# Gated feed-forward rows turned in blocks of 32 by 32 by VectorE, instead of by TensorE

## The chip, the cores and the metric

The kernel runs on one core of one Trainium2 chip. The metric is the device time of one execution in microseconds; the median of several runs counts. The engines named below are TensorE (PE in the profile; PEld is its weight load), VectorE (DVE), ScalarE (ACT), GpSimd (POOL) and SyncE (SP), which only issues DMAs here. Operands lie in SBUF, matmul results in PSUM, which has eight banks of 512 fp32 values on each of 128 partitions.

## The reference

Two transformer-like blocks, one behind the other, over 256 tokens with 2048 channels, in fp32. The first has two layers, each with a mixer, a cross-attention and a gated feed-forward. Only the feed-forward matters here:

```python
FFN_HIDDEN = ((8 * D_MODEL + 3 * 256 - 1) // (3 * 256)) * 256     # 5632

def swiglu(h, w_in, w_out):
    g, u = jnp.split(h @ w_in, 2, axis=-1)
    return (jax.nn.silu(g) * u) @ w_out

# in each of the 2 layers of the first block
x = x + swiglu(rms_norm(x, norm_ffn[i]), ffn_w_in[i], ffn_w_out[i])
```

## The kernel before

Every linear layer is done in split precision: a weight tile w becomes w_hi (rounded to fp32r, by ScalarE, L388) and w_lo = w - w_hi (by VectorE, L395), and activations are split likewise. Three products are added up: hi x w_hi, lo x w_hi (L949) and hi x w_lo (L956). Weights come in units of 2 x 128 rows by 512 columns (512 KB), loaded by SP (L376). Four slots (NS = 4) of w_raw, w_hi and w_lo go round: while TensorE works on unit u, ScalarE and VectorE make w_hi and w_lo of unit u + 4 as soon as TensorE has released unit u (semaphore w_used), and SP loads into a w_raw slot once VectorE's split of it is done (w_lo_done). One unit is 8 matmuls with w_hi and 4 with w_lo.

The first half of the feed-forward, `fin0` and `fin1`, runs over 11 blocks of 512 hidden columns (NH = 11) in each of the two layers. A block is 16 units: eight for the gate (b = 0, PSUM banks 0 and 1), eight for the up projection (b = 1, banks 2 and 3). Behind the gate ScalarE writes silu of it to sg (L995). Behind the block VectorE multiplies it with the up projection into hid (L1025): tokens on the partitions, 2 x 512 values each. The second half, `fout0` and `fout1`, needs the hidden columns on the partitions, so hid is turned. That happens one block later, beside the matmuls of the next block: TensorE turns the eight 128 x 128 tiles of hid into banks 4 and 5 after unit 2 of the gate (`transposes`, L918 to L925), ScalarE copies them out rounded to hidT_hi behind its split of unit 4 (`hi_part`, L976), and VectorE makes hidT_lo behind its own (`lo_part`, L1007). The semaphores are hid_done, ht_done (turned), ht_hi_done and ht_lo_done. Block 0 is written out; blocks 1 to 10 are one hardware loop on each engine (`turn_c`). What is left over of block 10 is handed to the next stage by `owed` and done at the given unit of it by `pay`, here in units 2 and 4 of the down projection; that one takes its unit j (b = 0) once ht_lo_done has reached block j // 2 + 1, so block 10's columns are wanted at units 20 and 21.

Each engine works through its instructions in order, so the order written in `pe_ffn`, `act_ffn` and `dve_ffn` is the order of execution.

Of the kernel before, what the change touches and what calls it, by code (L numbers as in the profile page):

```python
# [12 lines left out]
P = 128  # L13
SEQ = 256
TB = SEQ // P
# [30 lines left out]
def program(nc, a):  # L46
    ctx = ExitStack()
    with ctx:
        def sem(name):
            return ctx.enter_context(nc.semaphore(name))  # L50
# [10 lines left out]
        def new(name, shape, dt=F32):  # L61
            off = top[0]
            top[0] += (4 * int(np.prod(shape)) + 31) // 32 * 32
            assert top[0] <= base + slab_bytes, (name, top[0] - base - slab_bytes)
            return at(name, shape, off, dt)
# [9 lines left out]
        hid = new("hid", [TB, CB])  # L75
# [48 lines left out]
        ident = new("ident", [P])  # L124
# [49 lines left out]
        ps = ctx.enter_context(nc.psum_tensor("ps", [P, 8, 512], F32))  # L174
# [32 lines left out]
        hid_done = sem("hid_done")  # L207
        ht_done = sem("ht_done")
# [140 lines left out]
        owed = dict(pe=[], act=[], dve=[])  # L349

        def pay(who, j):
            for at_, work in owed[who]:
                if at_ == j:
                    work()
            owed[who] = [(at_, work) for at_, work in owed[who] if at_ != j]
# [34 lines left out]
        def dve_split(dve, us, i=0, body=0, first=False):  # L390
            v = us if first else us + NS
            if v >= NU:
                return
            dve.wait_ge(w_hi_done, v + 1 + i * body)
            nc.vector.tensor_tensor(w_lo[:, v % NS], w_raw[:, v % NS], w_hi[:, v % NS].bitcast(F32),  # L395
                                    ALU.subtract).then_inc(w_lo_done, 1)
# [28 lines left out]
        def tiles(t, k_off=0):  # L425
            return lambda k, tb: t[:, k + k_off, tb * P:(tb + 1) * P]
# [425 lines left out]
        def dve_add_out(dve, name, turned, mid=None):  # L852

            li = L[name]
            pool = name == "pool"

            def evac(i, b, used):
                e = block_no(name, i, b)
                dve.wait_ge(w_used, used)
                if pool:  # L860
                    dve.wait_ge(pscale_in, 16)
                if not (pool and b < 2):

                    dve.wait_ge(x_copied, XB0[name] + e - 1)
                c0 = b * CB if pool else li.cols(i)[b]
                xb = x[:, :, bass.ds(c0, CB)]
                if pool:
                    sc = pscale[:, c0:c0 + CB].rearrange("p (o n) -> p o n", o=1).broadcast_to([P, TB, CB])
                    vlink(nc.vector.tensor_tensor(stg[b % 2][:], acc(half_of(name, b)), sc, ALU.mult))
                    nc.vector.tensor_tensor(stg[b % 2][:], xb, stg[b % 2][:], ALU.add).then_inc(stg_done, 1)  # L870
                else:
                    nc.vector.tensor_tensor(stg[b % 2][:], xb, acc(half_of(name, b)), ALU.add).then_inc(stg_done, 1)
                dve.wait_ge(stg_done, XB0[name] + e + 1)
                dve.sem_inc(acc_free[half_of(name, b)], 1)
            split_turns(dve, dve_split, name, evac, mid, turn_x=lambda i, b: dve_turn_x(dve, name, turned, i, b))
# [28 lines left out]
        NH = HID // CB  # L904

        def turn_c(eng, l, body):

            body(0, True)
            with eng.Fori(1, NH) as i:
                body(i, False)  # L910
# [3 lines left out]
        def pe_ffn(pe, l):  # L914
            li = L[f"fin{l}"]
            h0 = NH * l

            def transposes(i):  # L918
                pe.wait_ge(hid_done, h0 + i)

                for j in range(4):
                    for h in range(TB):
                        mm = nc.tensor.transpose(ps[:, 4 + j // 2, (j % 2) * SEQ + h * P:(j % 2) * SEQ + (h + 1) * P],  # L923
                                                 hid[:, h, j * P:(j + 1) * P], ident[:])
                mm.then_inc(ht_done, 1)  # L925

            def body(i, first):
                for b in range(2):
                    if b == 0:
                        if first:  # L930
                            pe.wait_ge(acc_free[0], half0[f"fin{l}"][0])
                        else:
                            pe.wait_ge(silu_done, h0 + i)
                    else:
                        if first:
                            pe.wait_ge(acc_free[1], half0[f"fin{l}"][1])
                        else:
                            pe.wait_ge(hid_done, h0 + i)
                    for j in range(li.units):
                        us = li.u0 + b * li.units + j  # L940
                        s = us % NS
                        pe.wait_ge(w_hi_done, us + 1 + i * li.body)
                        if first and b == 0:
                            pe.wait_ge(t_lo_done, TS[f"ffn{l}"][0] + j + 1)
                        for kk in range(UK):
                            k = UK * j + kk
                            for tb in range(TB):
                                for part, lhs in enumerate((actT_hi, actT_lo)):
                                    nc.tensor.matmul(  # L949
                                        ps[:, 2 * b + tb], lhs[:, k, tb * P:(tb + 1) * P],  # L950
                                        w_hi[:, s, kk * CB:(kk + 1) * CB], start=(k == 0 and part == 0), stop=False)
                        pe.wait_ge(w_lo_done, us + 1 + i * li.body)
                        for kk in range(UK):
                            k = UK * j + kk
                            for tb in range(TB):
                                mm = nc.tensor.matmul(  # L956
                                    ps[:, 2 * b + tb], actT_hi[:, k, tb * P:(tb + 1) * P],
                                    w_lo[:, s, kk * CB:(kk + 1) * CB], start=False, stop=(k == KT - 1))
                        mm.then_inc(w_used, 1)
                        if b == 0 and j == 2 and not first:  # L960
                            transposes(i)
                        if b == 0 and first:
                            pay("pe", j)
            turn_c(pe, l, body)
            owed["pe"].append((2, lambda: transposes(NH)))
            pe.wait_ge(silu_done, h0 + NH)
            pe_linear(pe, f"fout{l}", tiles(hidT_hi), tiles(hidT_lo), ht_lo_done, lambda b, j: h0 + min(NH, j // 2 + 1),
                      turned=AFTER_FFN[l])
# [32 lines left out]
        def dve_ffn(dve, l):  # L1001
            li = L[f"fin{l}"]
            h0 = NH * l

            def lo_part(i):
                dve.wait_ge(ht_hi_done, h0 + i)
                nc.vector.tensor_tensor(hidT_lo[:, bass.ds(4 * i - 4, 4)],  # L1007
                                        ps[:, 4:6].rearrange("p b (j t) -> p (b j) t", j=2),
                                        hidT_hi[:, bass.ds(4 * i - 4, 4)].bitcast(F32), ALU.subtract)\
                    .then_inc(ht_lo_done, 1)  # L1010

            def body(i, first):
                for b in range(2):
                    for j in range(li.units):
                        dve_split(dve, li.u0 + b * li.units + j, i, li.body)
                        if b == 0 and j == 4 and not first:
                            lo_part(i)
                        if b == 0 and first:
                            pay("dve", j)
                dve.wait_ge(silu_done, h0 + 1 + i)  # L1020
                dve.wait_ge(w_used, li.u0 + (i + 1) * li.body)
                if not (l == 0 and first):
                    dve.wait_ge(ht_done, h0 + i)
                for tb in range(TB):
                    ins = nc.vector.scalar_tensor_tensor(out=hid[:, tb], in0=ps[:, 2 + tb], scalar=rx[:, tb:tb + 1],  # L1025
                                                         in1=sg[:, tb], op0=ALU.mult, op1=ALU.mult)
                ins.then_inc(hid_done, 1)
            turn_c(dve, l, body)
            owed["dve"].append((4, lambda: lo_part(NH)))
            dve_add_out(dve, f"fout{l}", AFTER_FFN[l])  # L1030

        i_turned = sem("i_turned")
# [1359 lines left out]
```

## Time and profile before

| | before |
|---|---|
| median of 3 runs | 3051.22 us (3050.28 to 3053.83) |
| profiled execution, its own time | 3052.06 us |
| its span | 3050.2 us |
| TensorE busy | 3014.4 us (99%) |
| VectorE busy | 1692.0 us (55%) |
| ScalarE busy | 1478.4 us (48%) |
| GpSimd busy | 276.0 us (9%) |
| granted TensorE clock, mean | 0.999 of full speed |

The span goes from the first to the last instruction. Busy time of an engine is the time in which at least one of its instructions runs; matmuls are pipelined, so their durations overlap, and how long one holds the queue is read from the distance of two starts. Idle time of an engine stands in brackets behind the instruction that ended it, with what released it.

### The profile page before, as it was taken

How to read it: one execution, taken by the hardware profiler on the slowest of the kernel's cores; microseconds unless marked ns; L12 is line 12 of the kernel's file. 1: busy time of each engine (PE TensorE's matmuls, PEld its weight loads, DVE VectorE, ACT ScalarE, POOL GpSimd, SP SyncE). 2: the span in 40 equal slices, each digit the busy share in tenths (PEclk: the TensorE clock that was granted, in tenths of full speed). 3: DMA queues.
4: the chain of work that ended last, by engine and by line, in shares of the span. 5: the costliest groups of instructions: out<-in, count | busy, mean ns of one | idle time of the engine just before them, and what ended most of it. 6: DMA issues, size and time to landing. Idle time of an engine off the chain costs nothing.

```text
span 3050.2 us, 38222 instructions
## 1 busy us (share of the span) xinstructions
PE 3014.4 (99%) x14184; PEld 2489.1 (82%) x14184; DVE 1692.0 (55%) x1778; ACT 1478.4 (48%) x1839; POOL 276.0 (9%) x269
## 2 busy tenths in 40 slices
PE   8999999999999999999999999999999999999999
PEld 7888888888888778888888888888887888888787
DVE  5654444544456855654444545457556555755654
ACT  6554444444445555544444444454555545455553
POOL 0110000000005421100000000004200000600000
PEclk9999999999999999999999999999999999999999
DMA  7666666666666546566666656566454455644455
GB/s 251 220 186 191 187 192 186 188 189 191 190 193 188 149 127 220 172 191 190 186 192 186 189 189 191 190 196 190 146 152 138 150 183 178 187 145 145 144 156 170
DMA packets 280736, 549.45 MB, mean 180 GB/s; under 512 B 16896, under 2 KB 18976, under 8 KB 280224
## 3 DMA queue, kind: packets, MB, share of 16 engines
q1 hardware_dynamic: 276352, 531.30, 57.7%
q0 software_dynamic: 4256, 16.40, 1.5%
q8 instruction: 85, 1.39, 0.2%
q14 instruction: 43, 0.35, 0.0%
HBM read 540.82 MB, written 6.82 MB: 180 GB/s over the span
## 4 chain that ended last, share of the span: by engine, by line
PE 93%; ACT 3%; DVE 2%; issue 1%; POOL 1%; DMA 1%; ACTq 0%; DVEq 0%; POOLq 0%
PE ps L454 22%; PE ps L949 21%; PE ps L510 13%; PE ps L462 11%; PE ps L956 10%; PE ps L481 7%; PE ps L1179 1%; PE ps L1090 1%; DVE w_lo L395 1%; ACT w_hi L388 1%; PE ps L1157 1%; PE ps L783 1%; PE ps L923 1%; PE ps L1065 1%; DMA w_raw<-xattn_w_kv 0%
## 5 line engine op out<-in xcount | busy, mean ns | idle before, releaser
L395 DVE TENSOR_TENSOR w_lo<-w_raw,w_hi 128x1024 fp32r<-128x1024 f32 x1008 | 1275.0, 1267 | 1314.6 <-ACT w_hi L388 1311.1
L388 ACT ACTIVATE w_hi<-w_raw 128x1024 fp32r<-128x1024 f32 x1008 | 1066.8, 1059 | 1466.7 <-PE ps L462 584.8
L949 PE MATMUL ps<-w_hi,actT_hi 128*128 128x512 f32 x1408 | 550.0, 391 | 0.0
L949 PE MATMUL ps<-w_hi,actT_lo 128*128 128x512 f32 x1408 | 547.9, 389 | 0.0
L510 PE MATMUL ps<-w_hi,actT_hi 128*128 128x512 f32 x960 | 389.5, 406 | 5.7 <-ACT pall L534 5.7
L956 PE MATMUL ps<-w_lo,actT_hi 128*128 128x512 f32 x1408 | 376.5, 389 | 0.0
L510 PE MATMUL ps<-w_hi,actT_lo 128*128 128x512 f32 x960 | 375.2, 391 | 0.0
L454 PE MATMUL ps<-w_hi,hidT_hi 128*128 128x512 f32 x864 | 319.5, 391 | 0.0
L956 PEld LDWEIGHTS ps<-w_lo,actT_hi 128*128 128x128 f32 x1408 | 264.3, 188 | 55.1
L949 PEld LDWEIGHTS ps<-w_hi,actT_lo 128*128 128x128 f32 x1408 | 264.4, 188 | 54.2
L949 PEld LDWEIGHTS ps<-w_hi,actT_hi 128*128 128x128 f32 x1408 | 264.4, 188 | 54.1
L454 PE MATMUL ps<-w_hi,hidT_lo 128*128 128x512 f32 x736 | 286.4, 389 | 0.0
L481 PE MATMUL ps<-w_lo,actT_hi 128*128 128x512 f32 x960 | 262.5, 390 | 0.0
L510 PEld LDWEIGHTS ps<-w_hi,actT_hi 128*128 128x128 f32 x960 | 180.8, 188 | 47.3 <-issue 9.4
L462 PE MATMUL ps<-w_lo,hidT_hi 128*128 128x512 f32 x800 | 214.0, 389 | 0.0
L481 PEld LDWEIGHTS ps<-w_lo,actT_hi 128*128 128x128 f32 x960 | 180.2, 188 | 39.0
L510 PEld LDWEIGHTS ps<-w_hi,actT_lo 128*128 128x128 f32 x960 | 181.0, 188 | 34.1 <-issue 0.5
L454 PEld LDWEIGHTS ps<-w_hi,hidT_hi 128*128 128x128 f32 x864 | 161.8, 188 | 33.3 <-issue 0.3
L462 PEld LDWEIGHTS ps<-w_lo,hidT_hi 128*128 128x128 f32 x800 | 150.2, 188 | 31.3
L454 PE MATMUL ps<-w_hi,actT_hi 128*128 128x512 f32 (+1 forms) x416 | 161.4, 388 | 2.1 <-ACT w_hi L388 2.1
L454 PEld LDWEIGHTS ps<-w_hi,hidT_lo 128*128 128x128 f32 x736 | 138.2, 188 | 28.3
L454 PE MATMUL ps<-w_hi,actT_lo 128*128 128x512 f32 (+1 forms) x416 | 160.4, 386 | 0.0
(299 smaller groups left out, 2835.3 us busy)
## 6 DMA issues: line engine op xcount, KB each, us to landing
w_raw<-ffn_w_in SPq DMA_DIRECT2D x352, 512.0 KB, 3.6
w_raw<-w_in SPq DMA_DIRECT2D x256, 512.0 KB, 3.6
w_raw<-ffn_w_out SPq DMA_DIRECT2D x176, 512.0 KB, 3.8
w_raw<-w_out SPq DMA_DIRECT2D x64, 512.0 KB, 3.7
w_raw<-attn_w_in SPq DMA_DIRECT2D x48, 512.0 KB, 3.7
w_raw<-xattn_w_kv SPq DMA_DIRECT2D x32, 512.0 KB, 6.1
w_raw<-attn_w_out SPq DMA_DIRECT2D x32, 512.0 KB, 3.7
w_raw<-xattn_w_q SPq DMA_DIRECT2D x16, 512.0 KB, 3.7
```

The lines of the kernel that those rows point to most:

```text
L388: nc.scalar.activation(w_hi[:, v % NS], w_raw[:, v % NS], ACT.Copy).then_inc(w_hi_done, 1)
L395: nc.vector.tensor_tensor(w_lo[:, v % NS], w_raw[:, v % NS], w_hi[:, v % NS].bitcast(F32), ALU.subtract).then_inc(w_lo_done, 1)
L454: nc.tensor.matmul(ps[:, 2 * half + tb, 0:li.width], lhs(ks[kk], tb), w_hi[:, s, c:c + li.width], start=(j == 0 and kk == 0 and part == 0) ...
L462: mm = nc.tensor.matmul(ps[:, 2 * half + tb, 0:li.width], hi(ks[kk], tb), w_lo[:, s, c:c + li.width], start=False, stop=(j == li.units - 1 ...
L481: mm = nc.tensor.matmul(ps[:, 2 * half + tb], hi(k, tb), w_lo[:, s, kk * CB:(kk + 1) * CB], start=False, stop=(k == KT - 1))
L510: nc.tensor.matmul(ps[:, 2 * half + tb], lhs(k, tb), w_hi[:, s, kk * CB:(kk + 1) * CB], start=(k == 0 and part == 0), stop=False)
L783: mm = nc.tensor.transpose(ps[:, 4 + 2 * p + c, o:o + P], stg[p][:, h, k * P:(k + 1) * P], ident[:])
L923: mm = nc.tensor.transpose(ps[:, 4 + j // 2, (j % 2) * SEQ + h * P:(j % 2) * SEQ + (h + 1) * P], hid[:, h, j * P:(j + 1) * P], ident[:])
L949: nc.tensor.matmul(ps[:, 2 * b + tb], lhs[:, k, tb * P:(tb + 1) * P], w_hi[:, s, kk * CB:(kk + 1) * CB], start=(k == 0 and part == 0), sto ...
L956: mm = nc.tensor.matmul(ps[:, 2 * b + tb], actT_hi[:, k, tb * P:(tb + 1) * P], w_lo[:, s, kk * CB:(kk + 1) * CB], start=False, stop=(k == ...
L1065: mm = nc.tensor.transpose(ps[:, psum + col // 512, col % 512:col % 512 + P], src, ident[:])
L1090: mm = nc.tensor.matmul(o, un["q"][h], un["k"][h], start=un["row"] is None, stop=un["row"] is None or h >= 2)
```

## The change

VectorE turns hid, TensorE no longer does. VectorE's transpose works on blocks of 32 x 32. One instruction takes the 32 tokens of one quarter a of the partitions and the 32 columns of quarter f of each 128-column tile (for 4 tiles and 2 halves of the tokens: 8 blocks), turns each block and writes it to the partitions of quarter f in banks 4 and 5, at the columns of quarter a. Four such instructions (f = 0 to 3) make a quarter, four quarters a block. The quarters stand behind VectorE's splits of units 0 to 3 of the next block; the last one raises ht_done. `lo_part` moves from behind the split of unit 4 to that of unit 6. ScalarE's `hi_part` stays where it is. VectorE no longer waits for ht_done before it writes hid. For the last block of a layer the quarters are handed to units 0 to 3 of the down projection, and `lo_part` to its unit 6.

```diff
@@ pe_ffn
-            def transposes(i):
-                pe.wait_ge(hid_done, h0 + i)
-
-                for j in range(4):
-                    for h in range(TB):
-                        mm = nc.tensor.transpose(ps[:, 4 + j // 2, (j % 2) * SEQ + h * P:(j % 2) * SEQ + (h + 1) * P],
-                                                 hid[:, h, j * P:(j + 1) * P], ident[:])
-                mm.then_inc(ht_done, 1)
-
...
-                        if b == 0 and j == 2 and not first:
-                            transposes(i)
                         if b == 0 and first:
                             pay("pe", j)
             turn_c(pe, l, body)
-            owed["pe"].append((2, lambda: transposes(NH)))
@@ dve_ffn
+            def turn_quarter(i, a):
+                if a == 0:
+                    dve.wait_ge(hid_done, h0 + i)
+                for f in range(4):
+                    ins = nc.vector.transpose(
+                        ps[32 * f:32 * f + 32, 4:6].rearrange("p b (k h t) -> p h (b k) t", k=2, h=TB)
+                        [:, :, :, 32 * a:32 * a + 32],
+                        hid[32 * a:32 * a + 32].rearrange("p h (k n) -> p h k n", k=4)[:, :, :, 32 * f:32 * f + 32])
+                if a == 3:
+                    ins.then_inc(ht_done, 1)
+
...
-                        if b == 0 and j == 4 and not first:
+                        if b == 0 and j < 4 and not first:
+                            turn_quarter(i, j)
+                        if b == 0 and j == 6 and not first:
                             lo_part(i)
...
-                if not (l == 0 and first):
-                    dve.wait_ge(ht_done, h0 + i)
...
-            owed["dve"].append((4, lambda: lo_part(NH)))
+            for a_ in range(4):
+                owed["dve"].append((a_, lambda a_=a_: turn_quarter(NH, a_)))
+            owed["dve"].append((6, lambda: lo_part(NH)))
```

## Rows read from the trace of the kernel before

**Rows 1.** The page: busy time, chain that ended last by engine, one load.
```profile
span 3050.2 us, 38222 instructions
PE 3014.4 (99%) x14184; PEld 2489.1 (82%) x14184; DVE 1692.0 (55%) x1778; ACT 1478.4 (48%) x1839; POOL 276.0 (9%) x269
PE 93%; ACT 3%; DVE 2%; issue 1%; POOL 1%; DMA 1%; ACTq 0%; DVEq 0%; POOLq 0%
w_raw<-ffn_w_in SPq DMA_DIRECT2D x352, 512.0 KB, 3.6
```

**Rows 2.** By stretch: busy us (instructions) of PE, PEld, DVE, ACT, POOL; clock; DMA share; GB/s.
```profile
224.00:662.00 438.00, 438.00 (x1974) 363.46 (x1973) 217.45 (x189) 188.32 (x188) 0.00 (x0) 1.00 0.65 189
662.00:853.00 191.00, 191.00 (x856) 158.44 (x855) 94.25 (x83) 76.98 (x78) 2.09 (x2) 1.00 0.61 191
1293.00:1730.00 437.00, 437.00 (x1970) 362.66 (x1969) 217.56 (x193) 190.06 (x190) 0.00 (x0) 1.00 0.65 190
1730.00:1920.00 190.00, 190.00 (x852) 157.56 (x851) 94.98 (x83) 78.10 (x81) 2.09 (x2) 1.00 0.60 190
```

**Rows 3.** TensorE in order of time, 228 to 236 us: start, duration, instruction.
```profile
228.79 1.07 PE L956 MATMUL ps<-w_lo,actT_hi 128*128 128x512 f32 x4
...
231.51 1.07 PE L956 MATMUL ps<-w_lo,actT_hi 128*128 128x512 f32 x4
232.42 1.03 PE L923 MATMUL ps<-ident,hid 128*128 128x128 f32 x8
...
235.12 1.07 PE L956 MATMUL ps<-w_lo,actT_hi 128*128 128x512 f32 x4
```

**Rows 4.** VectorE in order of time, first layer; in brackets idle time before.
```profile
181.41 1.66 DVE L818 SCALAR_TENSOR_TENSOR actT_lo<-ps,gcols,actT_hi 128x256 fp32r<-128x256 f32 x4
...
226.75 1.40 DVE L1025 SCALAR_TENSOR_TENSOR hid<-ps,rx,sg 128x512 f32<-128x512 f32 x2
228.27 1.23 DVE L395 TENSOR_TENSOR w_lo<-w_raw,w_hi 128x1024 fp32r<-128x1024 f32 x1
...
240.04 1.23 DVE L395 TENSOR_TENSOR w_lo<-w_raw,w_hi 128x1024 fp32r<-128x1024 f32 x1 [1.49 <-ACT w_hi L388]
241.18 1.22 DVE L1007 TENSOR_TENSOR hidT_lo<-ps,hidT_hi 128x1024 f32 x1
242.76 1.23 DVE L395 TENSOR_TENSOR w_lo<-w_raw,w_hi 128x1024 fp32r<-128x1024 f32 x1 [0.36 <-ACT w_hi L388]
```

**Rows 5.** All instructions of line 923: duration ns min/median/max, first and last start.
```profile
L923 PE MATMUL ps<-ident,hid x176: 270/272/273, 232.4 to 1774.0; 128*128 128x128 f32 x176
```

**Rows 6.** VectorE in order of time, second layer, the last two blocks' hid.
```profile
1723.11 1.40 DVE L1025 SCALAR_TENSOR_TENSOR hid<-ps,rx,sg 128x512 f32<-128x512 f32 x2
...
1767.53 1.40 DVE L1025 SCALAR_TENSOR_TENSOR hid<-ps,rx,sg 128x512 f32<-128x512 f32 x2
```

**Rows 7.** VectorE's groups by shape: count, busy us, mean ns of one.
```profile
L1486 DVE COPY pall<-ps 128x256 f32<-128x256 f32 x8 | 3.3, 417 | 0.0
L818 DVE SCALAR_TENSOR_TENSOR actT_lo<-ps,gcols,actT_hi 128x256 fp32r<-128x256 f32 x80 | 33.1, 476 | 0.0
L641 DVE TENSOR_SCALAR xn<-x,rr 128x2048 f32<-128x2048 f32 x2 | 2.5, 1284 | 0.0
L630 DVE TENSOR_SCALAR nv<-ss 128x2 f32<-128x2 f32 x10 | 1.6, 165 | 2.3 <-ACT xn L601 2.3
L1860 DVE RECIPROCAL rr<-rt 128x32 f32<-128x32 f32 x6 | 2.1, 344 | 0.0
L1186 DVE RECIPROCAL rsum<-sums 128x4 f32<-128x4 f32 x24 | 4.0, 168 | 0.0
```

**Rows 8.** ScalarE in order of time, 225 to 250 us.
```profile
227.17 1.07 ACT L388 ACTIVATE w_hi<-w_raw 128x1024 fp32r<-128x1024 f32 x1 [1.60 <-PE ps L956]
...
239.91 1.01 ACT L976 ACTIVATE hidT_hi<-ps 128x1024 f32 x1
```

**Rows 9.** SyncE's waits, 224 to 760 us: us in total, times, longest us.
```profile
SPq L376 <- DVE w_lo L395: 413.8, 193, 3.0
```

## The prediction

> **What bounds the kernel now.** I read the page first [rows 1]. TensorE is busy 99% of the span at the full 2.4 GHz level, and holds 93% of the chain that ended last; VectorE is busy 55%, ScalarE 48%, so VectorE has room on average. An average says nothing about one stage, so the second view was the busy time by stretch [rows 2]: both stretches of the loop over hidden columns (224 to 662 us and 1293 to 1730 us), and both stretches of the down projection behind it, show TensorE busy without a gap, VectorE for 217.45 of 438 us. Whatever is taken off TensorE's queue there comes off the end, unless a wait grows in its place. The third view, TensorE's instructions in order of time [rows 3], shows what the transposes cost it. A unit is 12 matmuls and takes 2.72 us (231.51 - 228.79, start of the low part to start of the next). The unit with the eight transposes takes 3.61 (235.12 - 231.51). The transposes start right behind the fourth L956 matmul and had waited for nothing: hid was written at 226.75 to 228.15 [rows 4].
>
> **What is removed.** The 0.27 us of one transpose [rows 5] is its latency, not its place in the queue; 176 times that would be 48 us and wrong. The place in the queue is 3.61 - 2.72 = 0.89 us for eight. The same over a whole block of 16 units, from one hid to the next: in the second layer 1767.53 - 1723.11 = 44.42 us [rows 6]; 16 x 2.72 = 43.52; the difference is 0.90 us. I take 0.90. There are 176 transposes [rows 5], in groups of eight: 22 groups (11 blocks in each of 2 layers; the 11th group of a layer stands in unit 2 of the down projection). 22 x 0.90 = 19.8 us, all on a path without gaps.
>
> The wait of VectorE for ht_done before it writes hid goes too. It cost nothing: TensorE's transposes follow hid by some 5 us [rows 3, 4] and the next hid comes only a block later.
>
> **What is added.** VectorE gets 16 transposes for each block, in four quarters behind the split (w_lo) of units 0 to 3. One instruction reads 32 partitions x 256 values of SBUF and writes 32 x 256 into PSUM. No row of before shows a VectorE transpose, nor VectorE writing PSUM. Bounds by rows [rows 7]: the cheapest per element is the one-source scalar operation, 1284 ns for 2048 values; at that slope from 165 ns for 2 values 256 values take 0.30 us. The dearest is the reciprocal, 344 ns for 32 values and 168 ns for 4, so 6.3 ns a value and 1.8 us for 256. The nearest in kind is the copy between PSUM and SBUF with one source and 256 values, 0.42 us, then the two-source operation of the same size, 0.48 us, which stands in the queue for (1.66 - 0.476)/3 = 0.39 us when four follow each other [rows 4]. I take 0.45 us a piece, as four in a row may not overlap like those; the range to keep is 0.30 to 1.8.
>
> The rows put one value at about 1 ns for an operation of this kind: 1.22 us for 1024 values [rows 4] against 0.417 for 256 [rows 7] is 1.04 ns a value. The Trainium skill has two rules here that point apart. Its table of rules for kernel authors (VectorE: DVE Perf Modes) gives a 128 x 128 transpose to TensorE and keeps VectorE for 32 x 32; its page Vector Engine (DVE) Microarchitecture Reference (section 3.8) has the 32 x 32 array sustain one element a cycle in each lane, and lets an instruction of at most 32 partitions write to any quarter. By the second, a piece costs what the copy costs and the sum below stands; by the first, the sixteen pieces are the dearer way, which is the first rival.
>
> **Where it goes on VectorE.** Zero is the moment when ScalarE starts w_hi behind unit 0, 227.17 [rows 8]. VectorE starts its split of unit 0 at +1.10 (228.27) and an operation behind a split can start 1.14 later (241.18 - 240.04) [rows 4]. So a unit costs VectorE 1.14 + 4t, with t the time of one piece: 2.94 us at 0.45, against TensorE's 2.72. It falls behind by 0.2 us a unit, for four units, and catches up afterwards. The last quarter ends at 1.10 + 4 x 1.14 + 16t = 5.66 + 16t = 12.9 us. Who waits for that:
> - ScalarE, in hi_part behind w_hi of unit 4, is ready at 4 x 2.72 + 1.07 = 12.0. It waits 0.9 us, then 1.01 for hi_part [rows 8], and starts the next w_hi at 13.9 instead of 13.6. Queued behind its wait are the w_hi of the units to come.
> - VectorE's own split of unit 4 is late by 1 us; lo_part moves from unit 4 to unit 6, and its reader, the down projection, wants the last block's part only at its unit 20.
> - SP's loads wait for a free w_raw, which VectorE's split releases [rows 9]: late by 1 us as well, with 3.6 us to land [rows 1].
>
> None of it reaches TensorE, because four slots are in flight. The split behind unit 0 makes w_lo of unit 4, wanted at 3 x 2.72 + 8 x 0.227 = 9.97 us. For the split behind unit 4, the worst one, it is 20.85, and it ends at 5.66 + 16t + 1.23 = 6.89 + 16t: 14.1 us at 0.45, 6.7 us early. ScalarE's w_hi of unit 9 ends at 5.66 + 16t + 1.01 + 1.07 = 7.74 + 16t and is wanted at 21.76. Both covers last to t = 0.87 us. A load let go at 14.1 lands at 17.7, and ScalarE wants it at 21.76; that cover is thinner (4 us) but ScalarE has 7 us more behind it. The added work on VectorE (16 x 0.45 x 22 = 158 us) is therefore costed at nothing.
>
> **The sum.** Profiled span 3050.2 - 19.8 = 3030.4; the profiled execution took 3052.06, 1.9 more than its span, so 3032.3. The median of the runs is 3051.22, 0.84 below that execution: 3031.4 us, 0.65% less. In the other stages nothing is edited, and the work before and behind moves up as a whole.
>
> **Rivals.**
> - A piece takes far more than a copy (slower). From t = 0.87 the queue of splits comes too late: TensorE stands in each block for 16 x (t - 0.87), 352 x (t - 0.87) us over both layers, and the balance is zero at t = 0.87 + 19.8/352 = 0.93 us. At four times the slope, 256 x 4.2 ns + 0.15 = 1.2 us, it gives 3031.4 + 116 = 3147 us; at the upper bound of 1.8 us some 3360. For it: the reciprocal shows that an operation here can cost six times as much a value, and these pieces are like no row in their pattern, with runs of 32 values, reads in one quarter and writes in another. Against it: the copy and the two-source operations of [rows 7] run at about 1 ns a value. Chance 0.09. By the Trainium skill's rate of one element a cycle this rival falls away; no row of before can show it.
> - Writing PSUM disturbs TensorE. VectorE now writes banks 4 and 5 while TensorE accumulates in 0 and 1. 352 pieces against 19.8 us: 0.056 us of lost matmul for each would eat the gain, half of it gives 3041 us. For it: no row shows the case. Against it: reads of PSUM by ScalarE and VectorE beside TensorE (L976, L1007) leave the unit at 2.72 us (240.04 to 242.76) [rows 4]. Chance 0.06.
> - The gain doesn't arrive at the end, since loads, w_hi or w_lo become the bound: no change, 3051 us. Against it: in the loop VectorE waits 1.49 us in most units [rows 4], and ScalarE does 1.07 us of work in 2.72 [rows 8]. Chance 0.03.
>
> **How the numbers follow.** Forecast 3031.4 with 0.82; within it the term can be off by 0.02 us a group (0.5 us) and the runs by 2 us, so 3029 to 3034. To leave out no more than 2 in 10, and to take in the half-eaten gain, the range goes from 3029 to 3043 us. This kernel's measurement tells some 0.2% (6 us) from no change. Faster by more: 0.82 + 0.05 of the second rival = 0.87. Within: 0.01 + 0.03 = 0.04. Slower: 0.09.
>
> **What the profile after would show.** No L923; every unit of the loop at 2.72 us, a block at 43.5. TensorE busy without a gap in the two loops. 352 transposes on VectorE at 0.40 to 0.50 us; its busy time up by about 150 us. ScalarE's L976 released by VectorE instead of standing behind its own w_hi, and its next w_hi up to 1 us late. The forecast is wrong if a piece lasts over 0.87 us, shown as TensorE waiting for w_lo or w_hi in units 8 and 9 of each block, or if matmuls beside the pieces start more than 0.227 us apart.

## The result and the profile after

The changed kernel takes 3031.59 us (median of 4 runs, 3028.01 to 3035.99) against 3051.46 us before (4 runs beside them, 3050.28 to 3053.83). The ratio is 0.9936 with a 95% interval of 0.9923 to 0.9948: 19.9 us less, where 19.8 were forecast (3031.4 us; range 3029 to 3043).

The page of after: span, busy times, chain, the new instruction's group and the median landing time of the weights.

```profile
span 3029.9 us, 38202 instructions
PE 2994.8 (99%) x14008; PEld 2470.8 (82%) x14008; DVE 1850.6 (61%) x2130; ACT 1478.4 (49%) x1839; POOL 275.2 (9%) x269
PE 93%; ACT 2%; DVE 2%; issue 1%; POOL 1%; DMA 0%; ACTq 0%; DVEq 0%; POOLq 0%
L998 DVE STREAM_TRANSPOSE ps<-hid 32x256 f32<-32x256 f32 x352 | 160.4, 456 | 6.3
w_raw<-ffn_w_in SPq DMA_DIRECT2D x352, 512.0 KB, 4.3
```

The busy time of TensorE fell by 19.6 us (3014.4 to 2994.8), the span by 20.3, and VectorE's busy time rose by 158.6 us against [rows 1]: the work changed its engine and became eight times dearer, and the end moved by what left TensorE alone.

After by stretch, the two hidden loops, which answer to the first and third line of [rows 2] (columns as there):

```profile
224.00:654.00 430.00, 430.00 (x1899) 356.06 (x1898) 290.25 (x349) 188.32 (x188) 0.00 (x0) 1.00 0.66 193
...
1284.00:1711.00 427.00, 427.00 (x1886) 353.56 (x1885) 284.00 (x344) 188.30 (x189) 0.00 (x0) 1.00 0.66 193
```

TensorE is still busy without a gap, VectorE now for 290 of 430 us. In the down projections behind the loops (654 to 842 us and 1711 to 1900 us) TensorE has no gap either. TensorE in order of time, the low parts of four units in a row, which answer to [rows 3]:

```profile
227.08 1.07 PE L947 MATMUL ps<-w_lo,actT_hi 128*128 128x512 f32 x4
...
229.80 1.07 PE L947 MATMUL ps<-w_lo,actT_hi 128*128 128x512 f32 x4
...
232.52 1.07 PE L947 MATMUL ps<-w_lo,actT_hi 128*128 128x512 f32 x4
...
235.24 1.07 PE L947 MATMUL ps<-w_lo,actT_hi 128*128 128x512 f32 x4
```

2.72 us each time, while VectorE writes its pieces into banks 4 and 5. Where [rows 3] had a unit of 3.61 us there is none. VectorE over the same stretch, which answers to [rows 4]:

```profile
226.56 1.23 DVE L395 TENSOR_TENSOR w_lo<-w_raw,w_hi 128x1024 fp32r<-128x1024 f32 x1
227.82 1.86 DVE L998 STREAM_TRANSPOSE ps<-hid 32x256 f32<-32x256 f32 x4
229.59 1.20 DVE L395 TENSOR_TENSOR w_lo<-w_raw,w_hi 128x1024 fp32r<-128x1024 f32 x1
230.82 1.86 DVE L998 STREAM_TRANSPOSE ps<-hid 32x256 f32<-32x256 f32 x4
232.69 1.22 DVE L395 TENSOR_TENSOR w_lo<-w_raw,w_hi 128x1024 fp32r<-128x1024 f32 x1
...
237.08 1.88 DVE L998 STREAM_TRANSPOSE ps<-hid 32x256 f32<-32x256 f32 x4
238.98 1.22 DVE L395 TENSOR_TENSOR w_lo<-w_raw,w_hi 128x1024 fp32r<-128x1024 f32 x1
241.10 1.23 DVE L395 TENSOR_TENSOR w_lo<-w_raw,w_hi 128x1024 fp32r<-128x1024 f32 x1 [0.89 <-ACT w_hi L388]
```

No idle time stands in brackets between 226.56 and 238.98: VectorE runs without a pause for four units, falls behind, and at 241.10 already waits for ScalarE again. Four pieces take 1.86 us, so they start (1.86 - 0.456)/3 = 0.468 us apart. ScalarE, which answers to [rows 8] (zero of the prediction's clock is 225.46 here):

```profile
236.34 1.06 ACT L388 ACTIVATE w_hi<-w_raw 128x1024 fp32r<-128x1024 f32 x1 [1.66 <-PE ps L947]
239.10 1.03 ACT L964 ACTIVATE hidT_hi<-ps 128x1024 f32 x1 [1.69 <-DVE ps L998]
240.02 1.05 ACT L388 ACTIVATE w_hi<-w_raw 128x1024 fp32r<-128x1024 f32 x1
```

It now waits 1.69 us for the last piece, and all 22 blocks do so, in the list of waits:

```profile
ACT hidT_hi L964 <- DVE ps L998: 36.9, 22, 1.7
```

None of that reaches TensorE: one block, from one hid to the next, takes 43.52 us.

```profile
268.50 1.40 DVE L1025 SCALAR_TENSOR_TENSOR hid<-ps,rx,sg 128x512 f32<-128x512 f32 x2
...
312.02 1.40 DVE L1025 SCALAR_TENSOR_TENSOR hid<-ps,rx,sg 128x512 f32<-128x512 f32 x2
```

The other blocks of both loops take the same to 0.06 us. Read this way, the trace is far finer than the medians of the runs.

### The profile page after: what moved, and what is told of

Its sections match the earlier page's. It is cut to its first block, busy times and chain, and to the rows that moved or that the text cites. A ratio compares the mean times of both kernels' runs of the same rounds, so it can differ in the third digit from the quotient of the medians.

```text
span 3029.9 us, 38202 instructions
## 1 busy us (share of the span) xinstructions
PE 2994.8 (99%) x14008; PEld 2470.8 (82%) x14008; DVE 1850.6 (61%) x2130; ACT 1478.4 (49%) x1839; POOL 275.2 (9%) x269
## 4 chain that ended last, share of the span: by engine, by line
PE 93%; ACT 2%; DVE 2%; issue 1%; POOL 1%; DMA 0%; ACTq 0%; DVEq 0%; POOLq 0%
PE ps L454 23%; PE ps L940 21%; PE ps L510 14%; PE ps L462 11%; PE ps L947 11%; PE ps L481 7%; PE ps L1181 1%; PE ps L1092 1%; DVE w_lo L395 1%; PE ps L1159 1%; PE ps L783 1%; ACT w_hi L388 1%; PE ps L1067 1%; PE ps L724 0%; PE ps L1205 0%
## 5 line engine op out<-in xcount | busy, mean ns | idle before, releaser
L462 PE MATMUL ps<-w_lo,hidT_hi 128*128 128x512 f32 x800 | 214.0, 389 | 0.0
L462 PEld LDWEIGHTS ps<-w_lo,hidT_hi 128*128 128x128 f32 x800 | 150.2, 188 | 31.4
L998 DVE STREAM_TRANSPOSE ps<-hid 32x256 f32<-32x256 f32 x352 | 160.4, 456 | 6.3
```

The source lines that it names most:

```text
L462: mm = nc.tensor.matmul(ps[:, 2 * half + tb, 0:li.width], hi(ks[kk], tb), w_lo[:, s, c:c + li.width], start=False, stop=(j == li.units - 1 ...
L998: ins = nc.vector.transpose(ps[32 * f:32 * f + 32, 4:6].rearrange("p b (k h t) -> p h (b k) t", k=2, h=TB) [:, :, :, 32 * a:32 * a + 32], ...
```

## Experiments

The theory: what a group of eight transposes held of TensorE's queue (0.90 us) is the whole gain; the 352 pieces are free as long as the split behind unit 4 is in time. Rival A: the pieces cost TensorE something, and the removal brought more than 0.90 us a group. Rival B: part of the gain is from the moved lo_part or the dropped wait. Where after is compared with a kernel of another group of runs, both stand against the kernel before of their own group.

### The pieces left out

```diff
             def turn_quarter(i, a):
-                if a == 0:
-                    dve.wait_ge(hid_done, h0 + i)
-                for f in range(4):
-                    ins = nc.vector.transpose(...)
-                if a == 3:
-                    ins.then_inc(ht_done, 1)
+                pass
...
-                act.wait_ge(ht_done, h0 + i)
+                act.wait_ge(hid_done, h0 + i)
...
-                                     ps[:, 4:6].rearrange("p b (j t) -> p (b j) t", j=2), ACT.Copy)\
+                                     hid[:].rearrange("p h (j t) -> p (h j) t", j=2), ACT.Copy)\
...
```

> The kernel after with the 352 pieces left out; nobody turns hid, and hi_part and lo_part read hid itself (so the hidden columns are not turned and the output is another). My theory (the pieces lie wholly in VectorE's idle time and disturb nothing): the same time as after, 3031.6 us, ratio 0.9935. Rival A (the pieces cost TensorE something by their writes to PSUM or by late w_lo, and TensorE's own transposes cost more than 0.90 us a group): clearly under after, say 3026 us or less. Rival B (part of the gain is from the moved lo_part or the dropped wait): can't show here, both are kept.

Measured: 3032.78 us, ratio 0.9937 (0.9924 to 0.9951), where after has 0.9936. Without a single piece the kernel is no faster, against rival A; the interval, 4 us to either side, leaves room for a small cost only. The trace narrows it down, by two hid in a row:

```profile
269.83 1.40 DVE L1019 SCALAR_TENSOR_TENSOR hid<-ps,rx,sg 128x512 f32<-128x512 f32 x2
...
313.35 1.40 DVE L1019 SCALAR_TENSOR_TENSOR hid<-ps,rx,sg 128x512 f32<-128x512 f32 x2
```

43.52 us, as in after: in the loops the sixteen pieces of a block cost nothing to 0.01 us.

### Both at once

```diff
+            def turn_quarter(i, a):
+                if a == 0:
+                    dve.wait_ge(hid_done, h0 + i)
+                for f in range(4):
+                    nc.vector.transpose(
+                        ps[32 * f:32 * f + 32, 6:8].rearrange("p b (k h t) -> p h (b k) t", k=2, h=TB)
+                        [:, :, :, 32 * a:32 * a + 32],
+                        hid[32 * a:32 * a + 32].rearrange("p h (k n) -> p h k n", k=4)[:, :, :, 32 * f:32 * f + 32])
...
-                        if b == 0 and j == 4 and not first:
+                        if b == 0 and j < 4 and not first:
+                            turn_quarter(i, j)
+                        if b == 0 and j == 6 and not first:
                             lo_part(i)
...
```

> The kernel before with TensorE's transposes kept and in use, and VectorE's 352 pieces added, written to banks 6 and 7 where nobody reads them; lo_part behind the split of unit 6 as in after; the wait of VectorE for ht_done kept. My theory: the time of before, 3051.5 us, ratio 1.000. Rival A: above before, by what e1 is under after. Rival B (the gain lies in the moved lo_part): under before.

Measured: 3052.22 us (11 runs), ratio 1.0002 (0.9993 to 1.0011). This is the tightest of the intervals: all 352 pieces and the moved lo_part together change the time by at most 0.11%, 3.4 us of the 20 that are to be explained. Rival A and the moved lo_part of rival B fall as explanations of the gain. TensorE in order of time, with VectorE at its pieces all the while:

```profile
231.06 1.08 PE L956 MATMUL ps<-w_lo,actT_hi 128*128 128x512 f32 x4
231.98 1.04 PE L923 MATMUL ps<-ident,hid 128*128 128x128 f32 x8
...
234.70 1.08 PE L956 MATMUL ps<-w_lo,actT_hi 128*128 128x512 f32 x4
```

3.64 us for the unit with the transposes, 3.61 in [rows 3]. The dropped wait was not in this kernel. The trace of before has the answer in the group of the instruction that stood behind that wait (its last number is the idle time before it, in us):

```profile
L1025 DVE SCALAR_TENSOR_TENSOR hid<-ps,rx,sg 128x512 f32<-128x512 f32 x44 | 30.9, 743 | 0.0
```

VectorE never idled there, so dropping the wait could give nothing back.

### One layer only

```diff
-                        if b == 0 and j < 4 and not first:
+                        if b == 0 and j < 4 and not first and l == 0:
                             turn_quarter(i, j)
...
+                        if b == 0 and j == 2 and not first and l == 1:
+                            transposes(i)
...
+                if l == 1:
+                    dve.wait_ge(ht_done, h0 + i)
...
```

> VectorE turns in the first layer only, TensorE in the second. My theory: 11 groups of 0.90 us, 9.9 us, so 3041.5 us, ratio 0.9968; blocks of 43.5 us in the first layer and of 44.4 in the second. A gain that came from one layer alone would give 3031.6 or 3051.5.

Measured: 3039.74 us, ratio 0.9961 (0.9948 to 0.9975), 1.8 us under the forecast of 3041.5, whose ratio 0.9968 lies inside the interval. hid in both layers of this kernel:

```profile
225.99 1.40 DVE L1040 SCALAR_TENSOR_TENSOR hid<-ps,rx,sg 128x512 f32<-128x512 f32 x2
...
269.45 1.40 DVE L1040 SCALAR_TENSOR_TENSOR hid<-ps,rx,sg 128x512 f32<-128x512 f32 x2
```
```profile
1712.48 1.40 DVE L1040 SCALAR_TENSOR_TENSOR hid<-ps,rx,sg 128x512 f32<-128x512 f32 x2
...
1756.89 1.41 DVE L1040 SCALAR_TENSOR_TENSOR hid<-ps,rx,sg 128x512 f32<-128x512 f32 x2
```

The block shown takes 43.46 us where VectorE turns and 44.41 where TensorE does, and the other blocks of each loop agree with it to 0.06 us: the difference, 0.90 to 0.95 us, is in each block of the layer that was edited and in none of the other.

### The removed work priced by itself

```diff
-                for j in range(4):
+                for j in (0, 1, 2, 3, 0, 1, 2, 3):
                     for h in range(TB):
                         mm = nc.tensor.transpose(...)
```

> The kernel before with each of TensorE's transposes done twice, to the same place. Prices the removed work by itself. My theory: eight more cost what eight cost in the queue, by the row of before (1.03 - 0.27)/7 = 0.108 us each, 0.87 us a group: 22 x 0.87 = 19 us more, 3070.5 us, ratio 1.0062. If their latency of 0.27 us counted it would be 48 us more, 3099 us.

Measured: 3070.63 us, ratio 1.0062 (1.0049 to 1.0076), 19.2 us over before: 0.87 us for each of 22 groups. The queue price, not the latency of 0.27 us each, which would have given 48 us.

```profile
231.49 1.08 PE L956 MATMUL ps<-w_lo,actT_hi 128*128 128x512 f32 x4
232.41 1.91 PE L923 MATMUL ps<-ident,hid 128*128 128x128 f32 x16
...
236.00 1.08 PE L956 MATMUL ps<-w_lo,actT_hi 128*128 128x512 f32 x4
```

Sixteen take 1.91 us instead of 1.03, and the unit 4.51 instead of 3.61. Adding the groups and taking them away move the end by nearly the same (19.2 and 19.9 us), so nothing else was late next on either side.

### Half as many pieces more

```diff
+                for f in (0, 1):
+                    ins = nc.vector.transpose(
+                        ps[32 * f:32 * f + 32, 6:8].rearrange("p b (k h t) -> p h (b k) t", k=2, h=TB)
+                        [:, :, :, 32 * ((a + 0) % 4):32 * ((a + 0) % 4) + 32],
+                        hid[32 * a:32 * a + 32].rearrange("p h (k n) -> p h k n", k=4)[:, :, :, 32 * f:32 * f + 32])
                 for f in range(4):
...
```

> After with 24 pieces a block instead of 16: in each quarter two of the four are done a first time into banks 6 and 7, where nobody reads them. With 0.468 us from one piece to the next and 1.26 for a split in front of them, as the trace of after has it, a unit costs VectorE 1.26 + 6 x 0.468 = 4.07 us, the split behind unit 4 ends at 1.10 + 4 x 4.07 + 1.23 = 18.6 us, and TensorE wants it at 20.85. My theory (four slots cover the lag up to that point): the time of after, 3031.6 us. Rival (every lag of VectorE costs TensorE something): 176 pieces more at a part of 0.468 us, 3040 us or more.

Measured: 3034.29 us, ratio 0.9940 (0.9926 to 0.9954). The median stands 2.7 us over after's, the ratios 0.0004 (1.2 us) apart and well within their intervals. TensorE has no wait for w_lo or w_hi in the feed-forward, and two hid in a row stand 43.52 us apart, as in after:

```profile
269.68 1.40 DVE L1030 SCALAR_TENSOR_TENSOR hid<-ps,rx,sg 128x512 f32<-128x512 f32 x2
...
313.20 1.40 DVE L1030 SCALAR_TENSOR_TENSOR hid<-ps,rx,sg 128x512 f32<-128x512 f32 x2
```

The rival's 3040 us is out. VectorE's busy time rose by 71 us (1850.6 to 1922.0 us) and the loops are no longer for it, so the 2.7 us between the medians don't come from them.

### Twice as many pieces

```diff
+                for f in range(4):
+                    ins = nc.vector.transpose(
+                        ps[32 * f:32 * f + 32, 6:8].rearrange("p b (k h t) -> p h (b k) t", k=2, h=TB)
+                        ...
                 for f in range(4):
...
```

> After with 32 pieces a block, each done a first time into banks 6 and 7. A unit costs VectorE 1.26 + 8 x 0.468 = 5.0 us; the split behind unit 4 ends at 1.10 + 20.0 + 1.23 = 22.3 us, wanted at 20.85. My theory: TensorE waits 1.5 to 1.7 us in each of 22 blocks for w_lo of unit 8, 33 to 37 us, so 3065 to 3069 us. Rival (VectorE's average decides, and it has room: 5.0 x 4 + 12 x 1.3 = 35.6 us of 43.5 a block): 3031.6 us.

Measured: 3072.17 us, ratio 1.0069 (1.0055 to 1.0083): 40.6 us over after, and slower than before. The list of TensorE's waits has two lines on the feed-forward, where after has none:

```profile
PE ps L947 <- DVE w_lo L395: 30.0, 20, 1.5
...
PE ps L462 <- DVE w_lo L395: 3.1, 2, 1.6
```

22 waits of 1.5 us, one a block (L462 is the down projection, with the last block's pieces of each layer). TensorE in order of time at unit 8 of a block:

```profile
290.38 1.07 PE L947 MATMUL ps<-w_lo,actT_hi 128*128 128x512 f32 x4
...
294.76 1.20 PE L947 MATMUL ps<-w_lo,actT_hi 128*128 128x512 f32 x4 [1.51 <-DVE w_lo L395]
...
297.63 1.07 PE L947 MATMUL ps<-w_lo,actT_hi 128*128 128x512 f32 x4
```

The place is the one forecast, unit 8, the slot that the split behind unit 4 fills. The size was forecast as 1.5 to 1.7 us a block and is 1.81, so the whole came out above the forecast too (3072 us, not 3065 to 3069): the unit with the wait takes 4.38 us, 1.66 too many, and the one behind it 2.87, 0.15 too many. Two hid in a row confirm it:

```profile
317.30 1.41 DVE L1030 SCALAR_TENSOR_TENSOR hid<-ps,rx,sg 128x512 f32<-128x512 f32 x2
...
362.62 1.40 DVE L1030 SCALAR_TENSOR_TENSOR hid<-ps,rx,sg 128x512 f32<-128x512 f32 x2
```

45.32 us instead of 43.52, 1.80 times 22 = 39.6 us. A stop costs a little more than the idle time that the profile shows for it. Of the 1.66 us, 1.51 are counted as idle. The other 0.15 us fit the way idle time is counted: it begins at the end of the last matmul, which lasts 0.39 us, where the next would have started after 0.23. A further 0.15 us goes to the next unit, while TensorE starts again. The rival (VectorE's average decides) is out. The busy time of one block, 272 to 317.3 us, columns as in [rows 2]:

```profile
272.00:317.30 45.30, 43.79 (x193) 35.94 (x192) 36.23 (x53) 18.83 (x19) 0.00 (x0) 1.00 0.61 185
```

VectorE was busy for 36.23 of 45.30 us and had 9 us to spare, and TensorE waited all the same. Its granted clock is 1.00, so the wait cost no clock.

### All sixteen behind one unit

```diff
-                        if b == 0 and j < 4 and not first:
-                            turn_quarter(i, j)
+                        if b == 0 and j == 0 and not first:
+                            for a in range(4):
+                                turn_quarter(i, a)
...
-                owed["dve"].append((a_, lambda a_=a_: turn_quarter(NH, a_)))
+                owed["dve"].append((0, lambda a_=a_: turn_quarter(NH, a_)))
```

> After with all 16 pieces behind the split of unit 0 instead of four behind each of units 0 to 3. The split behind unit 1 ends at 1.10 + 1.26 + 7.5 + 1.23 = 11.1 us and is wanted at 12.69. My theory: 3031.6 us, the spreading over four units is not needed at this price. Rival (one long lag costs where four short ones do not): more than 3034 us.

Measured: 3031.07 us, ratio 0.9931 (0.9918 to 0.9945), the time of after. VectorE, then ScalarE:

```profile
228.62 7.50 DVE L998 STREAM_TRANSPOSE ps<-hid 32x256 f32<-32x256 f32 x16
236.16 4.63 DVE L395 TENSOR_TENSOR w_lo<-w_raw,w_hi 128x1024 fp32r<-128x1024 f32 x4
```
```profile
241.29 1.06 ACT L388 ACTIVATE w_hi<-w_raw 128x1024 fp32r<-128x1024 f32 x1 [2.17 <-DMA w_raw<-ffn_w_in]
```

VectorE does nothing else for 7.5 us and then four splits in one go. The late splits let the loads go late, and ScalarE waits 2.17 us for one. It has 40 such waits for ffn_w_in, 66.3 us in all, where after has none; the cover of w_hi takes that too. The spreading over four units is not what makes the pieces free.

### Pieces that stay in their quarter

```diff
-                        ps[32 * f:32 * f + 32, 4:6].rearrange("p b (k h t) -> p h (b k) t", k=2, h=TB)
-                        [:, :, :, 32 * a:32 * a + 32],
+                        ps[32 * a:32 * a + 32, 4:6].rearrange("p b (k h t) -> p h (b k) t", k=2, h=TB)
+                        [:, :, :, 32 * f:32 * f + 32],
```

> After with each piece written back to the quarter it was read from (the same four pieces of 32 x 256 values a quarter, so the blocks land in the wrong place and the output is another). One look, for the distance of the starts: if the change of quarter is what keeps a piece from starting beside the last one's end, pieces now start 0.39 us apart as the four operations of L818 do; if 0.468 us is the price of the transpose itself, they stay at 0.468. The time stays 3031.6 us either way.

Measured once: 3030.29 us. The group, and VectorE in order of time:

```profile
L998 DVE STREAM_TRANSPOSE ps<-hid 32x256 f32<-32x256 f32 x352 | 126.5, 424 | 2.7
```
```profile
228.26 1.23 DVE L395 TENSOR_TENSOR w_lo<-w_raw,w_hi 128x1024 fp32r<-128x1024 f32 x1
229.51 1.43 DVE L998 STREAM_TRANSPOSE ps<-hid 32x256 f32<-32x256 f32 x4
```

Four take 1.43 us instead of 1.86; they start (1.43 - 0.424)/3 = 0.335 us apart instead of 0.468 (0.39 was expected). The edit changed two things, though: a piece no longer writes another quarter than it reads, and four pieces in a row no longer write four different quarters. The second piece of quarter a = 1 tells the two apart. It reads quarter 1 and writes quarter 1 in both kernels; in after the piece in front of it wrote quarter 0, here quarter 1. The first two pieces of that quarter, in after and then here:

```profile
230.82 0.91 DVE L998 STREAM_TRANSPOSE ps<-hid 32x256 f32<-32x256 f32 x2
```
```profile
232.23 0.78 DVE L998 STREAM_TRANSPOSE ps<-hid 32x256 f32<-32x256 f32 x2
```

In after the two stand end to end (0.91 us, 0.45 each); here the second starts before the first has ended. So it is the change of the written quarter from one piece to the next that costs 0.13 us a piece, over a quarter of its price, and not the move within a piece. Without it the transpose is as cheap as the operations of [rows 4] and [rows 7] at 256 values. This agrees with the Trainium skill (VectorE: DVE Perf Modes, section on two Vector instructions with no wait between them): an instruction whose output starts in another quarter of the partitions than the last output into the same memory waits until the earlier ones have finished. In after a piece starts 0.468 us behind one that lasts 0.456; here 0.335 behind one of 0.424. This mean is of two kinds: the first of each four, behind a split, lasts 0.45 to 0.47 us as in after, the other three 0.40 to 0.42.

### The same for other transposes

```diff
+        def by_dve(name, i, b):
+            return name in BY_DVE and 2 * i + b < 3
+
+        def turn_stg(dve, name, i, b, a):
+            p = b % 2
+            if a == 0:
+                dve.wait_ge(stg_done, XB0[name] + 2 * i + b + 1)
+            for f in range(4):
+                ins = nc.vector.transpose(
+                    ps[32 * f:32 * f + 32, 4 + 2 * p:6 + 2 * p].rearrange("p b (k h t) -> p h (b k) t", k=2, h=TB)
+                    [:, :, :, 32 * a:32 * a + 32],
+                    stg[p][32 * a:32 * a + 32].rearrange("p h (k n) -> p h k n", k=4)[:, :, :, 32 * f:32 * f + 32])
+            if a == 3:
+                ins.then_inc(t_done, 2)
...
-                        if turned and j == li.units - 1:
+                        if turned and j == li.units - 1 and not by_dve(name, i, b):
```

> After, and in both down projections the sums of the first three of four output blocks (256 tokens by 512 columns each) are turned by VectorE too, in 16 pieces behind the splits of units 0 to 3 of the next block, ScalarE's copies behind unit 4, VectorE's behind unit 6; the fourth block, whose turned rows the next stage wants at once, stays with TensorE. 6 groups of eight transposes leave TensorE's queue. My theory: 6 x 0.90 = 5.4 us less than after, 3026.2 us, ratio to before 0.9917. Rival (here VectorE first adds the block, 1.2 us, and GpSimd copies it beside, so the lag passes what four slots cover): 3031.6 us or more.

Measured: 3025.43 us, ratio 0.9913 (0.9900 to 0.9927). With the output projection as well (BY_DVE has "out0" too):

> As e9, and the same for three of the four blocks of the output projection of the first layer of the second half (8 units a block, so the copies at units 4 and 6 stand close to the end of the block). My theory: 9 x 0.90 = 8.1 us less than after, 3023.5 us, ratio to before 0.9908. Rival: as e9 or slower, if the lag of a block of only 8 units runs into its own adding.

Measured: 3024.0 us, ratio 0.9907 (0.9892 to 0.9923). Both ratios are those expected (0.9917, 0.9908) within their intervals, but intervals of that width touch those of after. So after and the second of the two ran once more, in the same rounds:

> After itself, unchanged, on the same chip and in the same rounds as the next kernel: 3031.6 us, ratio 0.9935.

> The kernel of e10 once more, beside after. If the 9 groups are worth 0.90 us each it stands 8.1 us (0.27%) under after in the same rounds; if e9's and e10's times were a difference between chips, it stands level with it.

Measured: after 3032.76 us (3030.9 to 3034.37), ratio 0.9936 (0.9922 to 0.9949); with the nine further groups 3024.63 us (3022.67 to 3025.56), ratio 0.9909 (0.9893 to 0.9924). That is 8.1 us less, 0.90 us a group, as expected, and no run of one lies among the runs of the other (the two intervals still touch, at 0.9922 to 0.9924). The version is faster than both kernels. The further pieces among its VectorE groups, 144 of them, cost 456 ns each like the others (from the trace of its first group of runs):

```profile
L409 DVE STREAM_TRANSPOSE ps<-sg 32x256 f32<-32x256 f32 x96 | 43.8, 456 | 1.7
L409 DVE STREAM_TRANSPOSE ps<-hid 32x256 f32<-32x256 f32 x48 | 21.9, 456 | 0.9
```

## Why the prediction was right

**The price of what is removed.** 0.90 us a group from the distance of starts. Taking it away brought 19.9 us over 22 groups, doubling it cost 19.2, nine more groups brought 8.1: 0.90, 0.87 and 0.90. The block of after is 43.52 us.

**The end moves by the whole of it.** TensorE was and is busy without a gap in the edited stages, and no new line stands in its list of waits. One layer gives about half: 11.7 of 19.9 us, where 9.9 were forecast, a difference within the interval, and by the blocks each layer gives its own part. That the total came within 0.1 us of the forecast is luck: the interval of the ratio is 3.8 us to either side.

**The price of a piece.** 0.45 us was taken, from the copy of the same size. It lasts 0.456 us. What the sum needs is the distance of starts, 0.468. The reason given, that four in a row may not overlap like those of L818, came true. The rows of before could not show why: each piece writes another quarter than the one in front of it, which adds 0.13 us to 0.335. A piece costs little more than the copy of 256 values (0.456 against 0.417 us), which is the second of the two rules that the prediction set against each other.

**The lag, the term that was mis-sized.** The prediction let a piece start 1.14 us behind the start of a split, as L1007 does in [rows 4]. In after it is 1.26 us (226.56 to 227.82), the split's whole duration and a little more. With the 0.02 us by which a piece was taken too cheap, a unit costs VectorE 3.0 to 3.1 us, not 2.94. The last quarter ends at 13.5 us, not 12.9 (238.96 - 225.46); ScalarE waits 1.7 us, not 0.9, and starts its next w_hi at 14.6, not 13.9. The split behind unit 4 ends at 14.7 us (238.98 + 1.22 - 225.46) and is wanted at 20.85, so 6.1 us of the forecast 6.7 us of cover are left, and it cost nothing here. It moves the point from which the pieces hurt: the split behind unit 4 ends at 1.10 + 4 x 1.26 + 16t + 1.23 = 7.37 + 16t, and the cover lasts to t = 0.84 us instead of 0.87. Twice the pieces is t = 0.94 and cost 40.6 us, one and a half times is t = 0.70 and cost nothing measurable; the limit lies between, as both formulas have it. The price beyond the limit was set too low: 352 x (0.936 - 0.87) gives 23 us for the doubled pieces. The longer lag adds 352 x 0.03 = 11 us, and the 0.3 us that each stop costs beyond its idle time adds 7, which makes 41. That the cover is a matter of one split's due time, not of VectorE's average, is shown by the pair.

**The rivals.** The dear piece didn't come. The prediction had the balance at zero at 0.93 us a piece; the doubled pieces, 0.94 us in its place, are 20.7 us slower than before, so the zero lies lower, between 0.84 (where the cover ends) and 0.94. Writes to PSUM beside TensorE cost nothing that shows: the unit stays at 2.72 us, and leaving the pieces out leaves the block at 43.52 us. That the gain would be lost to loads, w_hi or w_lo is refuted by the time itself.

**The moved lo_part and the dropped wait.** The kernel with both turns has the moved lo_part and stands level with before. The dropped wait alone wasn't tried; in the trace of before VectorE has no idle time at that place.

## What to carry to other kernels

Where one engine's queue is full from end to end, its work may go to an engine that does it eight times slower, as long as each thing that the slower engine owes is still on time. Work that out for the single worst item (when it ends, when it is wanted, how many slots lie between), not from busy shares: here twice the pieces left VectorE idle for a good part of each block and still cost more than the whole change had brought. And price removed work by the distance of the starts around it, never by the duration of one pipelined instruction.

## What the runs showed of the hardware

- A VectorE transpose of 32 partitions x 256 fp32 values, from SBUF to PSUM and from one quarter of the partitions to another, lasts 0.456 us, 0.468 from start to start, when each writes another quarter than the one before it; when they write the same quarter they start 0.335 us apart. The move within a piece has no price that shows: a piece that stays in its quarter, behind one that wrote another, takes as long as those that move.
- Behind a split a piece starts 1.26 us after the split's start in after, and 1.25 in the kernel whose pieces stay in their quarter, where L1007 started 1.14 us after it [rows 4]. In both kernels the piece behind a split writes another quarter than the piece before it did.
- A stop of TensorE that the profile shows as 1.51 us of idle time cost 1.81 us of the block.
- The median time of a 512 KB load of ffn_w_in to land was 3.6 us in [rows 1], 4.3 in after and 4.3 with all sixteen pieces in one go. It doesn't follow the pieces: it was 3.6 again with both turns, with all 352 pieces in place, and 3.9 with none. It cost nothing in any of these kernels, and what moves it stays open.
